# Layer norms along channels: raw x multiplied at once and corrected at the eviction, in a decoder layer on one core

## The reference, cut to what matters

```python
def layer_norm(x, g, b):
    x32 = x.astype(jnp.float32)
    mu = x32.mean(-1, keepdims=True)
    var = jnp.square(x32 - mu).mean(-1, keepdims=True)
    return ((x32 - mu) * lax.rsqrt(var + LN_EPS) * g + b).astype(x.dtype)
...
xp = layer_norm(ALPHA * xp + 0.5 * swiglu(xp, ffn1_w_gu, ffn1_w_down), ln_g[l, 0], ln_b[l, 0])
qa, ka, va, qr, kr, vr, gr, ga, gb = split(xp @ w_in)        # attention and retention follow
...
xp = layer_norm(ALPHA * xp + m @ w_out, ln_g[l, 1], ln_b[l, 1])
a, u = split(xp @ ffn2_w_gu)
xp = layer_norm(ALPHA * xp + 0.5 * (silu(a) * u) @ ffn2_w_down, ln_g[l, 2], ln_b[l, 2])
```

## Time and profile before

| what | us |
|---|---|
| median of 3 runs | 1923.88 (1921.61 to 1924.16) |
| the profiled execution, its own time | 1933.34 |
| its span, first to last instruction | 1931.1 |
| TensorE busy | 1796.5 (93%) |
| VectorE, ScalarE, GpSimd busy | 780.2, 668.2, 85.3 |
| granted TensorE clock, mean | 0.961 of 2.4 GHz |

### The profile page before, as it was taken

One profiled execution on the slowest core, in us unless ns is written; L12 is line 12 of the kernel. 1 busy time (PEld: TensorE's weight loads), 2 busy tenths in 40 slices (PEclk: granted clock), 3 DMA queues, 4 the chain that ended last, 5 costly groups with the idle time before them and its releaser, 6 DMA issues.

```text
span 1931.1 us, 32720 instructions
## 1 busy us (share of the span) xinstructions
PE 1796.5 (93%) x13119; PEld 1687.8 (87%) x13119; DVE 780.2 (40%) x1082; ACT 668.2 (35%) x899; POOL 85.3 (4%) x113
## 2 busy tenths in 40 slices
PE   5999999998998776999979999899999899999996
PEld 5999999987997545888869999669998799999996
DVE  2333332234323775777753223244344433333123
ACT  3333331124223555677743222123322433332111
POOL 0000000000001420000000000210000000000002
PEclk9999999998998997999989999889999999999998
DMA  4222223231431015788742232242222122222221
GB/s 140 87 87 87 87 87 98 82 94 38 134 113 44 1 30 174 268 275 300 269 131 66 77 109 66 75 154 88 87 88 87 35 88 89 88 88 84 85 98 46
DMA packets 146665, 203.84 MB, mean 106 GB/s; under 512 B 5538, under 2 KB 127330, under 8 KB 146594
## 3 DMA queue, kind: packets, MB, share of 16 engines
q1 hardware_dynamic: 145442, 198.35, 31.6%
q0 software_dynamic: 1152, 4.46, 0.6%
HBM read 191.39 MB, written 11.40 MB: 105 GB/s over the span
## 4 chain that ended last, share of the span: by engine, by line
PE 86%; DVE 5%; ACT 4%; issue 3%; DMA 0%; SPq 0%; POOL 0%; POOLq 0%; DVEq 0%; ACTq 0%
PE ps L295 68%; PE ps L1187 3%; PE ps L1208 2%; PE ps L1230 2%; PE ps L972 1%; PE ps L986 1%; PE ps L1635 1%; PE ps L1627 1%; PE ps L612 1%; PE ps L1246 1%; DVE vp_lo L1325 1%; DVE kt_lo L1304 1%; PE ps L697 1%; ACT vp_hi L1321 1%; ACT aT L1067 1%
## 5 line engine op out<-in xcount | busy, mean ns | idle before, releaser
L295 PE MATMUL ps<-xh,w_hi_t 128*128 128x272 f32 x2432 | 510.0, 291 | 25.6 <-DVE xl L649 18.2
L295 PE MATMUL ps<-xh,w_lo_t 128*128 128x272 f32 x2432 | 505.3, 289 | 0.0
L295 PE MATMUL ps<-xl,w_hi_t 128*128 128x272 f32 x2432 | 504.1, 289 | 0.0
L281 DVE TENSOR_TENSOR w_lo_t<-w_raw,w_hi_t 128x2048 fp32r<-128x2048 f32 (+1 forms) x112 | 252.4, 2254 | 519.2 <-ACT w_hi_t L277 519.2
L295 PEld LDWEIGHTS ps<-xh,w_hi_t 128*128 128x128 f32 x2432 | 384.5, 190 | 30.4 <-issue 21.1
L295 PEld LDWEIGHTS ps<-xl,w_hi_t 128*128 128x128 f32 x2432 | 385.0, 190 | 0.0
L295 PEld LDWEIGHTS ps<-xh,w_lo_t 128*128 128x128 f32 x2432 | 382.2, 190 | 0.0
L277 ACT CAST w_hi_t<-w_raw 128x2048 fp32r<-128x2048 f32 (+1 forms) x112 | 209.9, 1874 | 277.2 <-PE ps L295 277.2
L295 PE MATMUL ps<-hh,w_lo_t 128*128 128x272 f32 x704 | 145.7, 288 | 0.0
L295 PE MATMUL ps<-hh,w_hi_t 128*128 128x272 f32 x704 | 145.5, 288 | 0.0
L295 PE MATMUL ps<-hl,w_hi_t 128*128 128x272 f32 x704 | 145.1, 288 | 0.0
(11 more groups left out here) (241 smaller groups left out, 2069.7 us busy)
## 6 DMA issues: line engine op xcount, KB each, us to landing
w_raw<-in_ffn_w_gu_dram SPq DMA_DIRECT2D x44, 1024.0 KB, 5.0
w_raw<-in_w_in_dram SPq DMA_DIRECT2D x32, 1024.0 KB, 5.7
k_page<-in_cache_k_dram SPq DMA_DIRECT2D x64, 512.0 KB, 4.7
v_page<-in_cache_v_dram SPq DMA_DIRECT2D x64, 512.0 KB, 4.4
w_raw<-in_ffn_w_down_dram SPq DMA_DIRECT2D x16, 1024.0 KB, 5.1
w_raw<-in_ffn_w_down_dram SPq DMA_DIRECT2D x8, 768.0 KB, 4.6
w_raw<-in_w_branch_a_dram SPq DMA_DIRECT2D x4, 1024.0 KB, 5.0
st_in<-in_state_ret_dram SPq DMA_DIRECT2D x8, 512.0 KB, 5.0
```

What stands on the lines that cost most here:

```text
L281: nc.vector.tensor_tensor(w_lo_t[:, j, 0:nk], w_raw[:, j, 0:nk], w_hi_t[:, j, 0:nk].bitcast(F32), ALU.subtract).then_inc(lo_split, 1)
L295: mm = nc.tensor.matmul(ps[:, bank + half, 0:HALF], w[:, j, k, w_cols], m[:, k0 + k, half * HALF:half * HALF + HALF], start=start and k == ...
```

## The change

It changes what stands between the products of both channel norms.

- **Raw product.** The K projection and the first four tiles of FFN2 up no longer wait for a normalised x. `xh`, `xl` hold gain * x, not yet centred or scaled (ScalarE L745, VectorE L796), made tile by tile during the product before. Two columns are added behind the tokens, minus the gain and the bias, so `xh`, `xl` have rows of 546 instead of 544 and the second half's matmul has 274 columns. The tile is corrected when it is evicted (`dve_fix`): a copy of the two columns (L814), plus mean * column (L817), times 1/sd (L820), and the other column as the bias of ScalarE's activation.
- **Sums grown early.** After the first two residual tiles a pivot, their mean for each token, is taken off all 8 tiles of `xT` (TensorE L708, ScalarE L738, VectorE L773, L776 x8). Squares are made by ScalarE for each residual tile (L744) and summed by GpSimd into `x_ssq` (L845, L848). TensorE multiplies ones by `x_sum` and by `x_ssq` once each, in front of k-step 5 of the first raw tile (`pe_stats`).
- **Hand-over reordered.** GpSimd centres `xT` (L852), VectorE scales it (L824). ScalarE and VectorE write the normalised `xh` (L760), `xl` (L829) during the last raw tile, each k-step after TensorE has read it (`freed`); V, or the second group of FFN2 up, waits for `xl` by k-step.
- **Bias on GpSimd.** `pool_bias` adds the bias to `xT` (L838), in `ln1` after the K copies, in `ln2` right behind the centring.
- The two rounds of FFN down and of `out_proj` are written out instead of looped, and the first round of FFN2 up stands apart from its loop.

The diff, cut to its core:

```diff
-        def gemm(bank, j, n, nk, mh_, ml_, k0=0, start=True, stop=True, tile_ready=None):
+        def gemm(bank, j, n, nk, mh_, ml_, k0=0, start=True, stop=True, tile_ready=None, extra=0, freed=None,
+                 between=None):
             for k in range(nk):
+                if between and k == 5:
+                    between()
...
+                        cols = HALF + extra * half
...
+            def pe_stats(self, pe):
+                pe.wait_ge(self.summed, KD * self.i + KD)
+                for a in range(2):
+                    nc.tensor.matmul(ps[:, 4 + a, 0:HALF], ones[:], x_sum[:, a * HALF:a * HALF + HALF],
+                                     start=True, stop=True)
+                pe.wait_ge(self.ssq, KD * self.i + KD)
+                for a in range(2):
+                    mm = nc.tensor.matmul(ps[:, 6 + a, 0:HALF], ones[:], x_ssq[:, a * HALF:a * HALF + HALF],
+                                          start=True, stop=True)
+                mm.then_inc(self.spread, 1)
...
+            def act_take(self, act, k, resid, r0):
+                act.wait_ge(resid, r0 + k + 5)
+                act.wait_ge(self.shifted, KD * self.i + KD)
+                act.wait_ge(self.ssq, KD * self.i + k)
+                nc.scalar.activation(x_sq[:], xT[:, k], ACT.Square).then_inc(self.squared, 1)
+                nc.scalar.mul(xh[:, k, 0:T], xT[:, k], self.gain(k)).then_inc(self.raw_hi, 1)
...
+            def dve_low(self, dve, k):
+                dve.wait_ge(self.y_hi, KD * self.i + k + 1)
+                nc.vector.scalar_tensor_tensor(xl[:, k, 0:T], xT[:, k], self.bias(k), xh[:, k, 0:T].bitcast(F32),
+                                               ALU.add, ALU.subtract).then_inc(self.x_lo, 1)
...
+            def pool_bias(self, pool):
                 for k in range(KD):
+                    pool.wait_ge(self.x_lo, KD * self.i + k + 1)
+                    nc.gpsimd.tensor_tensor(xT[:, k], xT[:, k], self.bias(k).broadcast_to([P, T]), ALU.add
+                                            ).then_inc(self.y, 1)
...
+                pool.wait_ge(self.moment, 3 * self.i + 2)
+                pool.wait_ge(self.raw_lo, (KD + 2) * (self.i + 1))
                 for k in range(KD):
+                    nc.gpsimd.tensor_tensor(xT[:, k], xT[:, k], x_mu[:], ALU.subtract).then_inc(self.centered, 1)
```

More of the change, by code:

```diff
@@ L377, in act_part @@
+            def act_part(self, act, folded=None, norm=None):
+                c = self.c
+                if folded:
+                    self.act_up(act, 0, folded)
+                with act.Fori(1 if folded else 0, KF // 2) as i:
+                    self.act_up(act, i)
                 c += FFN_UP
+                if norm:
+                    norm.act_columns(act)
                 for q in range(2):
@@ L607, in pe_part @@
                                           start=True, stop=True)
-                mm.then_inc(self.mean, 1)
-                for k in range(KD):
-                    pe.wait_ge(self.squared, KD * self.i + k + 1)
-                    for a in range(2):
-                        mm = nc.tensor.matmul(ps[:, 2 + a, 0:HALF], ones[:], x_sq[:, k % 2, a * HALF:a * HALF + HALF],
-                                              start=k == 0, stop=k == KD - 1)
-                    mm.then_inc(self.sq_used, 1)
@@ new lines, in sums_read, with act_columns @@
+            def sums_read(self, pe, n):
+                if n == 0:
+                    pe.wait_ge(self.moment, 3 * self.i + 2)
+                else:
+                    pe.wait_ge(self.scale_set, 2 * self.i + 1)
+            def act_columns(self, act):
+                nc.scalar.activation(sd[:, 1:2], guard[:], ACT.Sqrt)
+                act.wait_ge(gemm_done, 4 + 2 * self.free_after)
+                nc.scalar.mul(xh[:, :, T:T + 1], ln_cols[:, self.i].unsqueeze(2), -1.0).then_inc(self.kept, 1)
+                nc.scalar.copy(xh[:, :, T + 1:T + 2], ln_cols[:, 2 + self.i].unsqueeze(2)).then_inc(self.kept, 1)
@@ new lines, in act_stats, with act_high @@
+            def act_stats(self, act):
+                act.wait_ge(self.spread, 2 * self.i + 2)
+                nc.scalar.activation(halves(x_msq[:]), banks(4), ACT.Square, scale=1.0 / D).then_inc(self.moment, 1)
+                nc.scalar.mul(halves(x_mu[:]), banks(4), 1.0 / D).then_inc(self.moment, 1)
+                act.wait_ge(self.scale_set, 2 * self.i + 1)
+                nc.scalar.activation(x_rs[:], x_rs[:], ACT.Sqrt, bias=guard[:]).then_inc(self.moment, 1)
+            def act_high(self, act, k, c):
+                act.wait_ge(self.scaled, KD * self.i + k + 1)
+                if k < KD - 1:
+                    act.wait_ge(self.freed, (KD - 1) * self.i + k + 1)
+                else:
+                    tile_done(act, c, 1)
+                nc.scalar.activation(xh[:, k, 0:T], xT[:, k], ACT.Identity, bias=self.bias(k)).then_inc(self.y_hi, 1)
```

461 lines of the change are left out of this document (325 added, 136 removed).

## The result

The changed kernel takes **1895.58 us** (median of 6 runs, 1894.47 to 1905.0) where the kernel before takes 1923.88 (6 runs, 1921.61 to 1925.39): ratio **0.9864**, 95% interval 0.9846 to 0.9883. That is 28.3 us less; the prediction said 31.8, and 1892.1 us. Unedited, on another chip beside some of the experiments, it gave 1895.59 against 1923.89 (0.9874, 0.9844 to 0.9903).

The account below looks back on a forecast made before the run. TensorE, busy 93% of the span, bounds the kernel; gains lie only where it stands still. 23.5 + 12.4 - 1.8 - 2.0 - 0.3 = 31.8 us, so 1923.9 becomes 1892.1 us, range 1877 to 1906; chance of this forecast 0.53.

Parts of the forecast that it names:

- second hand-over: Output projection's last matmul to FFN2 up's seventh tile: 12.4 us gained, before 2.0 us for the clock.
- three signs of being wrong: L829 back to back, a matmul reading `xh` at other than 125 ns, or over 5 us wait before k-step 5.
- First hand-over: FFN1 down's last matmul to K's third tile: start moves from 41.2 to 17.7 us behind it, 23.5 us gained.
- from the second on each alternates with a bias addition: FFN2's eight low parts on VectorE: six turns of 1.53 us with GpSimd, two of 0.77, last at +39.1.
- wait ahead of k-step 5: TensorE waits for GpSimd's last sum of squares after the output projection, from +3.8 to +5.6 us.
- the wait for the split: Before FFN2 up's seventh tile TensorE waits 5.5 us for the next chunk's weight split, ready at +51.5.
- Exclusion itself: GpSimd and VectorE take turns unless VectorE reads PSUM, a pair costing about 1.5 us; absent, +12.6 us gain.
- Rival 1: No collision: GpSimd's operations slip between VectorE's in both hand-overs; gain 44.4 us, 1879.5 us; chance 0.17.
- Rival 2: More collides: the reciprocal too excludes GpSimd, gain 28.6 us, 1895.3; with further losses 19.3, 1904.6; chance 0.22.
- Small costs: Two pivots on TensorE's path, 2 x 0.9 us; two extra columns in 12 tiles, 0.3 us; unrolled loops nothing.
- The low clock: Behind the wait before FFN2 up's seventh tile: clock granted 0.50 for 4 us, costing 2.0 us.
- Rival 3: Slower: rows of 546 start off 64-byte multiples, 7296 matmuls pay; at 12 ns each 88 us, 1980 us; chance 0.05.

## Why the prediction was right, and where it was not

- **Chance and range.** 1895.58 lies in 1877 to 1906, 3.5 us above the forecast. That is closer than the terms were, and luck: the second hand-over was 4.9 better, a term of 12.2 was missing, and 3.7 us of the medians aren't accounted for. Of the prediction's three signs of being wrong two came: L829 ran back to back, and a matmul reading `xh` took 127 ns.
- **First hand-over: right in each step.** Statistics, reciprocal, correction and turn stood within 0.4 us of their places. Only the wait's owner was off: `x_sum` 1.44 and `x_ssq` 0.44, where 2.7 for `x_ssq` was written, since VectorE's low part, in turn with GpSimd's sum, held the last sum on VectorE.
- **Second hand-over: the step that failed is "from the second on each alternates with a bias addition".** It carried single turns over to a row of eight. The low parts went back to back instead, and GpSimd's first addition took 5748 ns (7947 with one more split behind them). Absence of a wait does not explain it by itself: in the earlier trace rows too VectorE's operation of 614.00 started before the one ahead had ended, and GpSimd got in. The cause is open. The last residual was late by 2.1, not 3.4, and there was no wait ahead of k-step 5, where 1.8 was written. From the same turns, put in the wrong place, came the wait for the split: 6.93 for 5.5. The run with the split moved removes it wholly, and the run with late additions takes 3.3 off it (4.0 with the clock; the prediction put all eight additions at 5.4).
- **Exclusion itself: right.** Rival 1 (no collision) falls with 1.67 and 1.43 us beside GpSimd against 0.72 and 0.78 without. Rival 2's exclusion by the reciprocal falls too. GpSimd's centring runs through it in the first hand-over:
```profile
439.85 11.67 POOL L852 TENSOR_TENSOR xT<-xT,x_mu 128x544 f32<-128x544 f32 x8 [2.49 <-ACT x_mu L750]
```
Eight additions in 11.67 us, where eight alone are 10.7 to 10.9 (1.34 forecast, 1.36 for L848); shut out by the reciprocal of 3.56 they would have needed over 14, and the additions within it took 1.35 or 1.36 each. VectorE: DVE Perf Modes of the Trainium skill (section Mode 2x_2P) gives both ports to single-source operations and names `tensor_scalar` and `tensor_copy`. The trace shows that the reciprocal may not be counted among them.
- **Small costs.** The pivots took 0.93 each (0.9). The low clock lasted from the end of the pause to 1508.9, 5.1 us, and cost 2.3, not 2.0: the seventh to the twelfth tile of FFN2 took 38.9 us, and 36.6 in the run with the split moved.
- **Rival 3 happened, at 1.67 ns a matmul.** Its mechanism was named, with a break-even of 4.4 ns and one price, 12 ns; "no row shows a dependence on the start" then set it to zero in the sum. Every tile of before starts at a multiple of 64 bytes, and so does the second half, 1088 being 17 x 64: it was no argument against. Taken matmul by matmul, the trace of before had a sign: the time from one start to the next goes from 120.8 to 129.2 ns with the matmul's place in the tile, in a pattern that repeats every four k-steps. The term should have had both ends in the range. It cost 12.2 us, 38% of the gain forecast.

## What to carry to other kernels

When an edit changes how a tile's rows lie in memory, measure the matmul's pace in a stretch where nothing else waits, before and after: 1.3% of TensorE's time is invisible in a timeline and was as large here as one hand-over. When the serial part of a norm has been hidden, look at the next thing in that engine's queue that TensorE waits for (here the next weight split) and put it ahead of what nobody waits for: one moved split gave 8.9 us. And lay out the collisions of two engines over their queues: turns measured on a pair of operations need not hold for a row of them, and here other operations paid than those that were expected to.

## What the runs showed of the hardware that was not expected

- The pace of a matmul of 272 fp32r columns follows where its moving rows start. In FFN1, over rows of 544: 125.3 ns at multiples of 64 bytes; 123.9 with `xh` 16 and `xl` 48 bytes behind one; 126.7 with 8 and 40; over `hh` and `hl` 128.8 with 4 and 36, 124.45 with 32 and 0, 125.0 with 16 and 48. Rows of 546 gave 126.95 and of 548 125.55, in FFN1 and FFN2. It is constant to 0.1 ns round after round. These are means: within a tile single matmuls lie 120.8 to 129.2 ns apart with rows of 544, and 123.2 to 135.1 with rows of 546, each at its place in every tile.
- The same shifted tiles ran at 123.9 ns in FFN1 and 125.0 in FFN2 (16 bytes), 126.7 and 128.3 (8 bytes). With unshifted tiles both stages agree. This is open.
- A GpSimd operation of 1.09 us took 5.75 and 7.95 behind a row of eight low parts, and behind them and a weight split, while a sum of two full tensors got in between two operations of VectorE. VectorE's own operations beside GpSimd cost up to 1.2 more each (1.88 for 0.71).
- Decoding's stretch of 446 us lies between 442.3 and 449.1 over twelve traces, though no edit moves its work (the pace of its matmuls over `xh` is worth 0.6 us), so an edit's 2 us in a single trace prove nothing about the program's time. Whether the execution or the layout makes the difference isn't shown; the change's two traces differ by 0.5.
